# Expert results scattered to token rows in place of a slot buffer with gathers, in a hybrid diffusion trunk step

## What is computed

```python
_, idx = lax.top_k(jnp.where(emask, sb, -jnp.inf), TOP_K)          # TOP_K = 2
w = jnp.take_along_axis(s, idx, axis=-1)
w = w / jnp.sum(w, axis=-1, keepdims=True)
gates = jnp.sum(jax.nn.one_hot(idx, N_EXPERTS) * w[..., None], axis=-2)
a = jnp.einsum('bsd,edf->bsef', h, w_gate)                          # d = 1024, f = 256
u = jnp.einsum('bsd,edf->bsef', h, w_up)
act = jax.nn.silu(a) * u * gates[..., None]
return jnp.einsum('bsef,efd->bsd', act, w_down)
```

## Time and profile before

| | |
|---|---|
| runs of the kernel | 1850.19 us median of 3 (1845.79 to 1851.17) |
| profiled execution | 1863.73 us, span 1861.9 us, mean granted TensorE clock 0.926 |
| PE busy | 1538.1 us (83%) |
| DVE, ACT, POOL busy | 27%, 21%, 12% |
| DMA | 444.88 MB, mean 239 GB/s |
| share of the chain that ended last | PE 77%, DVE 8%, DMA 5%, issue 4%, ACT 3%, POOL 1% |
| in that chain | gathers of `y_slots` 2%, stores to `y_slots` 2% |

### The profile page before, as it was taken

One profiled execution on the slowest core, in us unless ns is written; L12 is line 12 of the kernel. 1 busy time (PEld: TensorE's weight loads), 2 busy tenths in 40 slices (PEclk: granted clock), 3 DMA queues, 4 the chain that ended last, 5 costly groups with the idle time before them and its releaser, 6 DMA issues.

```text
span 1861.9 us, 27291 instructions
## 1 busy us (share of the span) xinstructions
PE 1538.1 (83%) x11429; PEld 928.6 (50%) x11429; DVE 504.3 (27%) x1129; ACT 385.8 (21%) x983; POOL 231.8 (12%) x292
## 2 busy tenths in 40 slices
PE   2999978998494896999588989799993989969990
PEld 1776755333383685433274456653333866853330
DVE  0126331111326513111222442311113056141113
ACT  1115221111212601111111342201112036011111
POOL 1030011100115011000101000111002030120001
PEclk8999989999697998999788999989996999979995
DMA  9796317999674044899848203269997620538973
GB/s 345 276 329 174 120 62 294 420 420 403 256 257 88 10 158 159 325 421 421 332 164 271 45 23 136 68 256 419 421 407 268 232 52 1 203 147 339 422 302 113
DMA packets 128852, 444.88 MB, mean 239 GB/s; under 512 B 12963, under 2 KB 54902, under 8 KB 104150
## 3 DMA queue, kind: packets, MB, share of 16 engines
q1 hardware_dynamic: 97206, 351.37, 49.1%
q0 software_dynamic: 24576, 87.86, 13.8%
q10 hardware_dynamic: 6944, 3.84, 0.7%
HBM read 393.35 MB, written 49.69 MB: 238 GB/s over the span
## 4 chain that ended last, share of the span: by engine, by line
PE 77%; DVE 8%; DMA 5%; issue 4%; ACT 3%; POOL 1%; SPq 0%; POOLq 0%; DVEq 0%; ACTq 0%
PE bank L1409 67%; PE bank L1559 3%; PE bank L1707 2%; DMA xn<-y_slots,row_of 2%; PE bank L1465 2%; DMA y_slots<-kT 2%; DMA ring<-in_w_mod 1%; DVE xn L1022 1%; PE bank L1719 1%; ACT pp L904 1%; POOL small L588 1%; DVE V L1386 1%; DVE V L1388 1%; DVE x L1389 1%; PE bank L1603 1%
## 5 line engine op out<-in xcount | busy, mean ns | idle before, releaser
L1409 PE MATMUL bank<-ring,pp 128*32 128x512 f32 x2640 | 484.4, 594 | 3.8 <-ACT pp L486 2.8
L1409 PE MATMUL bank<-work,pp 128*32 128x512 f32 x1056 | 281.8, 599 | 0.9 <-DVE pp L1325 0.9
L1409 PE MATMUL bank<-ring,hT 128*128 128x256 f32 (+3 forms) x1142 | 263.7, 392 | 7.0 <-DVE kT L1221 2.6
L1409 PEld LDWEIGHTS bank<-ring,hT 128*128 128x128 f32 x1142 | 210.6, 193 | 58.5 <-issue 26.2
L1409 PEld LDWEIGHTS bank<-ring,pp 128*32 128x32 f32 x2640 | 123.0, 110 | 194.1 <-issue 187.3
L1409 PE MATMUL bank<-V,pp 128*32 128x512 f32 x912 | 167.3, 611 | 3.2 <-DVE pp L1325 3.2
L1409 PE MATMUL bank<-ring,xn 128*128 128x256 f32 x768 | 166.8, 380 | 0.0
L1409 PEld LDWEIGHTS bank<-ring,xn 128*128 128x128 f32 x768 | 145.6, 190 | 19.8
L1465 PE MATMUL bank<-ident,xn 128*128 128x128 f32 x192 | 39.5, 397 | 99.4 <-DVE xn L1022 99.4
L1341 DVE TENSOR_TENSOR pp<-bank,pp 128x256 f32<-128x256 f32 x48 | 20.4, 424 | 364.7 <-ACT pp L976 364.7
L1409 PE MATMUL bank<-ring,condT 128*32 128x256 f32 x1536 | 107.0, 418 | 11.6 <-DMA ring<-in_w_mod 7.2
(11 more groups left out here) (220 smaller groups left out, 1625.4 us busy)
## 6 DMA issues: line engine op xcount, KB each, us to landing
ring<-in_w_mod SPq DMA_DIRECT2D x96, 1024.0 KB, 11.2
ring<-in_moe_w_down SPq DMA_DIRECT2D x52, 1024.0 KB, 16.0
ring<-in_moe_w_gate SPq DMA_DIRECT2D x29, 1024.0 KB
ring<-in_moe_w_up SPq DMA_DIRECT2D x29, 1024.0 KB, 11.1
y_slots<-kT POOLq DMA_DIRECT2D x48, 512.0 KB, 8.2
hT<-h_slots POOLq DMA_DIRECT2D x44, 512.0 KB, 11.7
V<-in_moe_w_gate SPq DMA_DIRECT2D x19, 1024.0 KB, 11.2
V<-in_moe_w_up SPq DMA_DIRECT2D x19, 1024.0 KB, 14.6
```

The lines of the kernel that those rows point to most:

```text
L1409: return pe.matmul(out, lhsT, rhs, start=start, stop=stop)
```

## The change

Each token's two picks get a row of their own in a new DRAM list `y_picks` of 768 rows: row 2t + k for pick k of token t. To know which slot goes where, the kernel makes an inverse list for each layer. `pick_at`, a DRAM list of one word for each of the 1536 slots, is reset to a number out of bounds (a store from `no_pick`, ahead of the gate loads). After `block_in(2)` POOL scatters the pick numbers (`pick_no`) into it at the tokens' slots by six indirect DMAs of one word per partition, waits, loads the list into `pick_of` (12 words per partition, one for each block), and waits. `block_out` is then an indirect scatter of the 128 rows in `ys` to the rows of `y_picks` that `pick_of` names; rows out of bounds are left out. At the end of the layer three plain loads of 1 MB bring, for each token block, both picks of each token (8 KB a partition) into `y_pair[b]`: in `V` for b = 0, 1, in `pp` for b = 2. ACT waits for a new semaphore `y_ready`, which POOL raises when the loads are issued (and the slow path, if taken, is done), and for the load. `y_picks` is cleared once, in layer 0, by a copy inside DRAM of 768 cleared rows of `h_slots`, which SP issues after the layer's weight loads; POOL waits for it before its first scatter to `h_slots`. One more constant is loaded at the start on ACT's queue, and DVE makes two small integer copies of it.

```diff
+        pick_at = nc.dram_tensor("pick_at", [E * SLOTS, 1], U32).ap()
+        y_picks = nc.dram_tensor("y_picks", [2 * NT, D], F32).ap()
...
+        y_pair = [V[:, 0:2, :], V[:, 2:4, :], squares_[:, 0:2 * D].rearrange("p (k n) -> p k n", k=2)]
...
+                if L == 0:
+                    sp.wait_ge(zeroed, 16 * E)
+                    sp.dma_start(y_picks, h_slots[0:2 * NT, :]).then_inc(y_reset, 16)
                 sp.wait_ge(o_ready, 8 * (L + 1))
...
+                pool.dma_start(pick_at.rearrange("(p b) n -> p (b n)", p=P), no_pick[:, :]).then_inc(picks_reset, 16)
                 load_gate(L, 0)
...
-                    pool.dma_start(y_slots[blk * P:(blk + 1) * P, :], ys[:, blk % 2, :]).then_inc(y_out[blk % 2], 16)
+                    nc.gpsimd.indirect_dma_start(y_picks, rows_at(pick_of[:, blk:blk + 1]), ys[:, blk % 2, :], None,
+                                                 bounds_check=last_pick, oob_is_err=False).then_inc(y_out[blk % 2], 16)
...
                 block_in(2)
+                pool.wait_ge(picks_reset, 16 * (L + 1))
+                for b in range(NB):
+                    for k in range(2):
+                        nc.gpsimd.indirect_dma_start(pick_at, rows_at(row_of[:, k, b:b + 1]), pick_no[:, k, b:b + 1],
+                                                     None, bounds_check=last_base,
+                                                     oob_is_err=False).then_inc(picks_out, 16)
+                pool.wait_ge(picks_out, 96 * (L + 1))
+                with nc.allow_non_contiguous_dma(reason="one word for each slot"):
+                    pool.dma_start(pick_of[:, :], pick_at.rearrange("(b p) n -> p (b n)", p=P)).then_inc(picks_in, 16)
+                pool.wait_ge(picks_in, 16 * (L + 1))
                 for blk in range(BLOCKS):
...
-                further_passes(pool, L, step, picked_beyond)
-                for b in range(NB):
-                    for k, dst in enumerate((y_sum, y_second)):
-                        nc.gpsimd.indirect_dma_start(dst[:, b, :], None, y_slots, rows_at(row_of[:, k, b:b + 1]),
-                                                     bounds_check=last_base, oob_is_err=False).then_inc(y_in[b], 16)
+                flag = further_passes(pool, L, step)
+                for b in range(NB):
+                    pool.dma_start(y_pair[b], y_picks[2 * b * P:2 * (b + 1) * P, :].rearrange("(p k) n -> p k n", k=2))\
+                        .then_inc(y_in[b], 16)
+                with pool.If(flag > 0):
...
+                pool.sem_inc(y_ready, 1)
...
+                    act.wait_ge(y_ready, L + 1)
+                    act.wait_ge(y_in[b], 16 * (L + 1))
+                    nc.scalar.mul(y_pair[b][:, 0, :], y_pair[b][:, 0, :], wk[:, 0, b:b + 1]).then_inc(y_scaled, 1)
```

More of the change, by code:

```diff
@@ L269, in build @@
         wsum = sb("wsum", [P, NB])
+        pick_no = ctx.enter_context(nc.sbuf_tensor("pick_no", [P, 2, NB], U32))
+        pick_of = ctx.enter_context(nc.sbuf_tensor("pick_of", [P, BLOCKS], U32))
+        no_pick = ctx.enter_context(nc.sbuf_tensor("no_pick", [P, BLOCKS], U32))
+        pick_f = sb("pick_f", [P, 2 * NB + BLOCKS])
         load = sb("load", [P, E])
@@ L331, in build @@
         lat_sq, lat_rstd, states, wr_ready, first_ready = (sem(s) for s in ("lat_sq", "lat_rstd", "states", "wr_ready", "first_ready"))
+        picks_made, picks_reset, picks_out, picks_in, y_ready, y_reset = (sem(s) for s in
+            ("picks_made", "picks_reset", "picks_out", "picks_in", "y_ready", "y_reset"))
         freed = {"v": freed_v, "a": freed_a, "p": probs, "w": wo_mul}
@@ L462, in dest, with further_passes @@
             raise KeyError(key)
-        def further_passes(eng, L, step, after=None, blocks=None):
+        def further_passes(eng, L, step, blocks=None):
             eng.wait_ge(over_ready, L + 1)
@@ L475, in further_passes @@
                         step(eng.snap(gone + q * E + e), q, e)
-                if after is not None:
-                    after(gone)
+            return flag
         def turned(odd, half):
@@ L741, in step @@
                     pool.sem_inc(ov_done, 1)
-                def picked_beyond(gone):
-                    for b in range(NB):
-                        for k, dst in enumerate((y_sum, y_second)):
-                            nc.gpsimd.indirect_dma_start(dst[:, b, :], None, y_beyond, rows_at(beyond_of[:, k, b:b + 1]),
-                                                         bounds_check=last_beyond,
+                flag = further_passes(pool, L, step)
[3 more added lines that the diff above has]
+                with pool.If(flag > 0):
+                    gone = pool.value_load(over[0:1, DEPTH + L:DEPTH + L + 1], min_val=0, max_val=STEPS * (DEPTH - 1))
+                    for b in range(NB):
+                        pool.wait_ge(y_in[b], 16 * (L + 1))
+                    for b in range(NB):
+                        for k in range(2):
+                            nc.gpsimd.indirect_dma_start(y_pair[b][:, k, :], None, y_beyond,
+                                                         rows_at(beyond_of[:, k, b:b + 1]), bounds_check=last_beyond,
                                                          oob_is_err=False).then_inc(ov_picked, 16)
                     pool.wait_ge(ov_picked, pool.snap(gone * 2 + 96))
-                further_passes(pool, L, step, picked_beyond)
-                for b in range(NB):
-                    for k, dst in enumerate((y_sum, y_second)):
-                        nc.gpsimd.indirect_dma_start(dst[:, b, :], None, y_slots, rows_at(row_of[:, k, b:b + 1]),
-                                                     bounds_check=last_base, oob_is_err=False).then_inc(y_in[b], 16)
+                pool.sem_inc(y_ready, 1)
             norm_power(2 * DEPTH)
@@ L1385, in _ @@
                     dve.wait_ge(y_scaled, 3 * L + b + 1)
[L1386 to L1389, removed]
+                    y = y_pair[b][:, 0, :]
+                    link(V_.scalar_tensor_tensor(out=y, in0=y_pair[b][:, 1, :], scalar=wk[:, 1, b:b + 1],
+                                                 in1=y, op0=ALU.mult, op1=ALU.add))
+                    link(V_.tensor_tensor(y, y, gbc[:, 1, COND[b], :], ALU.mult))
+                    V_.tensor_tensor(x[:, b, :], x[:, b, :], y, ALU.add).then_inc(x_moe_v, 1)
             norm_scale(2 * DEPTH)
```

19 lines of the change are left out of this document (12 added, 7 removed).

## The result

The changed kernel takes 1860.59 us (median of 5 runs, 1858.84 to 1865.99), the kernel before beside it 1848.65 us (5 runs, 1845.79 to 1851.17). The ratio is 1.0064, 95% interval 1.0048 to 1.0080: **slower by 12 us**, where 1840.7 and faster was forecast. The changed kernel was slower on two of four occasions; on the other two it was level with the kernel before, as the experiments show. The profiled execution of the changed kernel took 1859.24 us (span 1857.5), close to its median; that of the kernel before took 1863.7, 15 us above its own. The two profiles therefore differ by 4 us in the wrong direction, and no total is read from their difference; durations inside them are.

What follows compares the result with a forecast made beforehand. PE was busy 83% of the span, with DMA engines full in the expert stage and layer 0's tail. Terms +2.0 - 5.2 - 11.5 + 5.2 = -9.5 us on median 1850.19 gave 1840.7; range 1830 to 1866, about 0.18 outside.

Steps and rivals of the forecast that it cites:

- (a): Last block's store becomes an indirect scatter that keeps POOL longer: +0.5 us in each tail, +2.0 in all.
- (b): Layer tails: three plain loads replace six gathers, -1.3 us a layer, -5.2 in all.
- (c): Empty slots not stored, 3 MB less a layer, shorter DMA queue in tails of layers 0 to 2: -11.5 us.
- (d): Pick words on POOL's queue delay block 3's load; PE stalls 3.2 us in layer 0, 2.0 in layer 1: +5.2.
- rival 3: DMA queue empties, so the byte saving counts whole, -23 us: 1829; chance 0.20.
- rival 1: Words late, each 4-byte piece taking turns with a weight packet; PE stalls in three layers: 1875; chance 0.17.
- Rival 2: Nothing to win: empty slots move anyway or next layer's weights refill the queue; byte saving 0: 1852; chance 0.24.
- Rival 4: Each block's scatter takes over 12.1 us and holds up POOL's loads, few us per block: above 1875; chance 0.03.

Runs made afterwards that it cites:

- d4: Changed kernel with block 3's load ahead of the wait for the words, and six indirect gathers in place of the three plain loads: 1864.58 us, ratio 1.0020.
- d2: Changed kernel with block 3's load issued ahead of the wait for the words, on an 1860 occasion: 1858.77 us, ratio 0.9984 to the kernel before.
- c3: Same kernel as d4 in another set: block 3's load ahead, six gathers in place of three loads: 1869.28 us, ratio 1.0049.
- b3: Changed kernel plus a plain store of 256 KB a block to a list nobody reads, putting the saved bytes back: 1871.03 us, ratio 1.0116.
- b1: Changed kernel, unedited, run again on an 1849 occasion: 1860.38 us, ratio 1.0070 to the kernel before.
- c4: Changed kernel with block 3's load ahead, plus a store of 256 KB a block to a list nobody reads: 1872.23 us, ratio 1.0063.
- b2: Changed kernel with block 3's load issued behind the words' six scatters, ahead of the wait for them, on an 1849 occasion: 1848.32 us, ratio 0.9999.
- e1: Changed kernel with the words' scatters issued behind block 3's load, and block 4's load ahead of the wait for them: 1861.95 us, ratio 1.0066.
- c2: Kernel before with the words made, brought back and not used, and block 3's load ahead of the wait for them: 1874.36 us, ratio 1.0081.
- c1: Control: kernel before, unedited, on an 1860 occasion: 1858.47 us, ratio 0.9997.
- d3: Changed kernel, unedited, on an 1860 occasion: 1860.23 us, ratio 0.9998 to the kernel before.
- e2: Control: kernel before, unedited, on an 1849 occasion: 1848.10 us, ratio 0.9992.
- a4: Changed kernel with the words' scatters ahead of the wait for the token scatter, and block 3's load ahead of the words' wait: 1884.67 us, ratio 1.0125.
- d1: Control: kernel before, unedited, on an 1860 occasion: 1860.63 us, ratio 0.9996.

## Why the prediction was wrong

**(a) Scatter for store: not measured alone.** Forecast +2.0. The last one changed by +0.29, +1.34, +0.79 and -1.51 us in layers 0 to 3, +0.9 in all, which holds the effect of the bytes as well.

**(b) Three loads for six gathers: right.** Forecast -5.2, measured -5.8 alone (d4 against d2; by c3, from another set, -10.5). The first load of results in layer 3 took 5.1 us for the pair's 6.38, the -1.3 of the sum.

**(c) Half the bytes: near in size, wrong in place.** Forecast -11.5, all of it in the tails of layers 0 to 2; measured -10.7 (b3 against b1) and -13.5 (c4 against d2). But layers 0 to 2 did not move towards layer 3's durations: the last scatters took 8.2 to 9.1 us there, and in layer 0 the engines stayed full at 400 GB/s until ACT began. The tails lose 6.5 to 8 us, and some 6 of that is (b): d4, which has (c) without (b), has tails of 220.2 us for d2's 214.3 and the kernel before's 221.6. c4's tails are 3.9 us longer than d2's; from the first to the last turnings it takes 489.8 us for 481.1. So most of what the bytes are worth lies between the blocks, where the queue is full and the words of (d) have just made a debt; what they are worth without the words was not tried. That the total came near is luck. I had added (c) to a kernel that was not delayed; b2, which has (a), (b), (c) and the words without the stall, only comes out level. So rival 3's premise, a queue that runs empty, never came about.

**(d) Pick words on POOL's queue: the step that failed.** Forecast +5.2, all of it PE waiting for block 3. Three things in it were wrong.

First, when PE asks for block 3. I read 334.7 and 781.6 off one profile that took 1863.7 us. In the changed kernel PE asked at 331.5 and 778.7, 3 us earlier, and so stood 5.3, 5.0, 1.5 and 1.4 us for my 3.2, 2.0, 0 and 0. Block 3 itself came as I had it: at 336.75 for 337.9, and at 783.65 for 783.6. That was luck, because errors cancelled. "The last begins near 310.7 and lands by the fastest load of the stage, 3.6 us" took a bound from below as the value; it landed 8.4 us after its start. The load of words, forecast 12.5, took 8.6. Together the words were there at 328.64 and not 326.8, and block 3's load then took 8.1 where I had 11.

Second, behind each of the first two stalls PE worked at the lower clock at first, another 2.0 and 2.2 us (a turning to turning of 14.14 and 14.26 in place of 12.10), which I had put at nothing. Stalls and clock are 17.4 us; b2 measures 12.1 for the edit that removes the stalls.

Third, what the words do to their neighbours had no term in the sum: 2304 words of 4 bytes travel in each layer, and words in a full queue hold back weights, as e1 shows. c2 prices words without stall at 14.7 us. The measured terms on an 1860 occasion are then 14.7 - 5.8 - 13.5 = -4.6 with block 3 ahead, where d2 gives -0.9; the 3.7 us between them hold (a) and the errors of three differences. On an 1849 occasion the stall stands on top: 12.

The rule that I weighed against the load of words, in the Trainium skill (DMA: Bandwidth & Descriptors, rules for kernel authors), that a strided last dimension becomes one descriptor for each element, is tested alone by no run here. The other rule, in the Trainium skill (DMA: Bandwidth & Descriptors, queues, rings and completion order), turns between queues by packets of several descriptors, fits the count of packets: POOL's queue has 25664 in c2 and 24576 in c1, 272 more a layer for the 2304 words and the reset of their list. A word is thus no packet of its own, as rival 1 had it. But that (d) would then be near 0 is not what e1's 61 to 123 GB/s show for such pieces.

**The rivals.** Rival 1 had the sign and the mechanism, words late and PE standing at block 3, but put the lateness on the load of words (over 16 us in the busy layers); that took 8.6 us at most in this trace and 12.9 in any (c3), and 1875 was too high. Rival 2's figure, 1852, misses, and its premise (c = 0) is refuted by b3 and c4; but of the tails it was right: they stay as full as before, as it said they would with the next layer's weights in the queue. Rival 4 did not occur.

**The start value.** I put the sum on the median of 1850.19 and the steps on a profile of 1863.7, and took the difference as a mere offset. It was not: the stall in layer 0 depends on when PE asks for block 3, at 331.98 in b2 and at 339.00 in d3, and on that profile it was 334.7. A profile 15 us above its kernel's median is no place to read a slack of 3 us from.

## What to carry to other kernels

Price a chain of tiny DMAs by its longest neighbours, not its shortest: scatters of 128 words could take as long to land as a store of 512 KB (8.4 and 7.9 us), and while they travelled they held up the megabytes behind them. Put what the busy engine wants next ahead of any wait in the same queue; that one line was worth 12 us where PE asked early (b2), and 1.5 where it was late anyway (d2 against d3). A saving on a full resource first pays the new debts on that resource, so count both in the same stage before taking either to the total.

## What the runs showed of the hardware

- Six scatters of 128 words of 4 bytes landed 4.0 (d3, layer 1) to 12.7 us (e1, amid a full queue) after the start of the last. In layer 3 the same kernel had 9.4 in one trace and 5.0 in another (b1). A load of 1536 such words landed in 3.4 (d3) to 12.9 us (c3) and cost POOL 1.08 us to issue.
- While they travel in a full queue the core's DMA falls from some 410 to 61 to 123 GB/s for 8 us, and a 1 MB weight load issued then lands in 18.7 us where it takes 9.4 without words (e2) and 13.8 with them ahead of the burst (b2).
- An indirect scatter leaves out rows with an index out of bounds: 12.5 MB fewer in the traffic of POOL's queue.
- Twelve indirect DMAs issued on POOL through PE's modulation products went with holes of 0.34 to 0.78 us on PE and a granted clock of 0.73 there (a4); six went with such holes in d1 and with none in e2.
- Behind stalls of 5.3 and 5.0 us PE first worked at the lower clock level (0.50 granted), so that they cost 2.0 and 2.2 us more than their length; behind those of 1.5 and 1.4 us it did not.
- The same program takes 1849 or 1860 us by occasion, even on one chip, and in the controls' traces the difference lies between a layer's second norm and the turning of its block 1, where such holes stand.
